# Half of a slot pair moved ahead of the row maxima, and fixed steps for the pairs of the sample attention

## What is computed

```python
h = rms_norm(x); q, k, v, u, g_att, g_s5 = split(h @ w_in)
att = softmax(q1 k1) v - lam * softmax(q2 k2) v        # 8 heads, causal; prompt, and sample over its pages
s5  = z * sigmoid(z @ w_glu + b_glu)                   # z = gelu(state space scan of u)
x   = x + (sigmoid(g_att) * (norm(att) @ w_pa) + sigmoid(g_s5) * (s5 @ w_ps)) @ w_out
# PEER: for every token and each of 8 heads, 16 experts out of 16384
h2  = rms_norm(x); s1, s2 = keys1 @ q1, keys2 @ q2      # 128 scores each; top 16 of each, top 16 of their sums
w   = softmax(best16) * gelu(dot(U[best16], h2))
x   = x + sum(w * V[best16]);  y = rms_norm(x)
```

## Time and profile before

| | |
|---|---|
| three runs | 4514.21, 4517.23, 4521.22 us |
| median | 4517.23 us |
| the profiled execution | 4512.55 us |
| its span in the trace | 4510.5 us |
| busy: PE, DVE, ACT, POOL | 74%, 67%, 33%, 30% of the span |
| DMA | 1418.40 MB, mean 314 GB/s |
| TensorE's mean granted clock | 0.90 of full speed |

### The profile page before, as it was taken

The page is one execution under the profiler, slowest core; times in us unless marked ns, Lnnn a source line. Parts: engine busy times, 40 slices in busy tenths (PEclk is TensorE's granted clock), DMA queues, the critical chain, the costliest instruction groups (busy, mean ns, idle before and its releaser), DMA issues. The chain is left out here.

```text
span 4510.5 us, 43431 instructions
## 1 busy us (share of the span) xinstructions
PE 3352.7 (74%) x13272; PEld 1915.2 (42%) x13272; DVE 3029.0 (67%) x6485; ACT 1502.6 (33%) x3882; POOL 1333.7 (30%) x1167
## 2 busy tenths in 40 slices
PE   7757979787768668877767758887777777777776
PEld 4636666543444344344456644442222222222221
DVE  6473021688887778967776667886666766666674
ACT  2121141233553214335433323323333333333332
POOL 0000000233223333422132323364444444434443
PEclk9877989898888889988878979999999999999999
DMA  3126425899878899966689989899999999999997
GB/s 128 24 1 112 148 83 179 334 377 351 283 262 340 333 393 359 405 223 224 217 320 389 402 328 395 315 397 419 420 418 412 414 412 414 410 414 397 413 409 306
DMA packets 285979, 1418.40 MB, mean 314 GB/s; under 512 B 47490, under 2 KB 89954, under 8 KB 148642
## 3 DMA queue, kind: packets, MB, share of 16 engines
q0 software_dynamic: 159344, 1129.94, 63.0%
q1 hardware_dynamic: 126018, 285.55, 18.4%
q10 hardware_dynamic: 384, 0.13, 0.0%
HBM read 1371.05 MB, written 42.11 MB: 313 GB/s over the span
## 5 line engine op out<-in xcount | busy, mean ns | idle before, releaser
L906 POOL DMA_INDIRECT arena<-in_uv,arena x1056 | 1265.2, 1198 | 2329.5 <-DVE arena L1017 1427.2
L1007 DVE CUSTOM_DVE_ANT_0 arena<-arena 128x1024 f32<-128x1024 f32 x1056 | 1289.0, 1222 | 491.0 <-DMA arena<-in_uv,arena 464.5
L1125 PE MATMUL ps<-arena 128*128 128x512 f32 (+1 forms) x2280 | 1079.0, 618 | 403.5 <-ACT arena L1094 403.5
L648 PE MATMUL ps<-arena 128*128 128x256 f32 (+2 forms) x3456 | 1111.0, 482 | 147.5 <-DMA arena<-in_w_stat 57.6
L648 PEld LDWEIGHTS ps<-arena 128*128 128x128 f32 x3456 | 685.5, 201 | 537.0 <-issue 350.3
L1125 PEld LDWEIGHTS ps<-arena 128*128 128x128 f32 (+1 forms) x2280 | 411.0, 190 | 1071.1 <-ACT arena L1094 625.0
L1075 ACT ACTIVATE arena<-arena 128x2 f32<-128x2 f32 x528 | 107.3, 203 | 1745.0 <-DVE arena L1007 1741.6
L1017 DVE SCALAR_TENSOR_TENSOR arena<-arena 128x1024 f32<-128x1024 f32 x486 | 622.3, 1280 | 10.3 <-ACT arena L1084 10.3
L1084 ACT ACTIVATE arena<-arena 128x1 f32<-128x1 f32 x1056 | 253.4, 287 | 17.6 <-ACT arena L1075 0.3
L1075 ACT ACT_TABLE_LOAD x158 | 202.7, 1283 | 10.5 <-PEq L1191 3.0
L1094 ACT ACTIVATE arena<-ident,arena 128x128 f32<-128x128 f32 x538 | 186.6, 394 | 8.8
(11 more groups left out here) (248 smaller groups left out, 3272.6 us busy)
## 6 DMA issues: line engine op xcount, KB each, us to landing
arena<-in_w_stat SPq DMA_DIRECT2D x216, 512.0 KB, 7.6
arena<-in_cache_k SPq DMA_DIRECT2D x64, 512.0 KB, 10.6
arena<-in_cache_v SPq DMA_DIRECT2D x64, 512.0 KB, 11.7
arena<-in_w_mov SPq DMA_DIRECT2D x14, 2048.0 KB, 14.3
arena<-in_uv,arena POOLq DMA_INDIRECT x1056, 13.0
arena<-in_x SPq DMA_DIRECT2D x16, 512.0 KB, 8.5
arena<-scr_s POOLq DMA_DIRECT2D x64, 128.0 KB, 12.9
scr_s<-arena SPq DMA_DIRECT2D x16, 384.0 KB, 12.0
```

The costliest lines, as they stand in the source:

```text
L648: last = nc.tensor.matmul(ps[:, bank, 0:w], wbuf[m % NWB][:, kc * P:(kc + 1) * P], moving[:, kc, :], start=(kc == 0), stop=(kc == KC - 1))
L906: pool.indirect_dma_start(ring[s % RING], None, dr["uv"], bass.IndirectOffsetOnAxis(ap=idx[:, g % 4, j:j + 1], axis=0)).then_inc(row_in[s ...
L1007: nc.vector.tensor_tensor_reduce(ring[s % RING][:, 0:D], ring[s % RING][:, 0:D], h2r[:, b % 2, :], 1.0, 0.0, ALU.mult, ALU.add, act_in[:, ...
L1125: last = nc.tensor.matmul(ps[0:m, 4 * (b % 2) + c, :], diag[:, n % 4, 0:m], ring[s % RING][:, D + 512 * c:D + 512 * (c + 1)], start=start, ...
```

## The change

Two edits. In the prompt attention a new `peer_dve_first` writes the first half of the unit's next pair (dot of slot 2p, add of slot 2(p-1)) right behind the probabilities, ahead of the maxima and of output_in; `peer_dve` later in the unit then leaves this half out. It does so in every unit, also in the last of a head, where no maxima follow. In the sample attention `share_dec` replaces `share`: five pairs per sequence of 8 steps, one each on steps 0, 1, 4, 6 and 7, so that all 40 stand on steps 0 to 63 and none behind. ScalarE's and VectorE's calls for pairs ahead of that go. GpSimd's list of pairs stays at all 40, at the start of the stage.

```diff
+        begun = {"dve": -1}
+
+        def dve_half(dve, p, q):
+            if p < PAIRS:
+                u_dot(dve, 2 * p + q)
+            if 0 < p <= PAIRS and not on_pe(p - 1):
+                v_add(dve, 2 * (p - 1) + q)
+
...
-            for q in range(2):
-                if p < PAIRS:
-                    u_dot(dve, 2 * p + q)
-                if 0 < p <= PAIRS and not on_pe(p - 1):
-                    v_add(dve, 2 * (p - 1) + q)
+            if begun["dve"] < p:
+                dve_half(dve, p, 0)
+            dve_half(dve, p, 1)
...
+        def peer_dve_first(dve, upto):
+            p = done_pairs["dve"]
+            if begun["dve"] < p < upto:
+                dve_half(dve, p, 0)
+                begun["dve"] = p
+
...
+        def share_dec(c, n):
+            before = PAIRS_BEFORE[c] + sum(PAIR_PLAN[c][:STAGES.index("dec")])
+            return before + min(PAIR_PLAN[c][STAGES.index("dec")], n // PAGES * 5 + (1, 2, 2, 2, 3, 3, 4, 5)[n % PAGES])
...
                             probabilities(h, i)
+                            peer_dve_first(dve, share(c, "att", h * nf + i + 1, H * nf))
                             if i + 1 < nf:
                                 maxima(h, i + 1)
...
-                        peer_pe(pe, share(c, "dec", n + 4, n_all))
+                        peer_pe(pe, share_dec(c, n))
...
-                    peer_act(act, share(c, "dec", 3, n_all))
...
-                        peer_act(act, share(c, "dec", n + 4, n_all))
+                        peer_act(act, share_dec(c, n))
...
-                        if n == 1:
-                            peer_dve(dve, share(c, "dec", 3, n_all))
...
-                        peer_dve(dve, share(c, "dec", n + 4, n_all))
+                        peer_dve(dve, share_dec(c, n))
...
-                    peer_pool(pool, share(c, "dec", 0, 1))
+                    peer_pool(pool, share_dec(c, N_STEPS - 1))
```

## The result

| | before | changed |
|---|---|---|
| median | 4516.40 us | 4537.46 us |
| four runs | 4514.21 to 4521.22 | 4535.84 to 4538.54 |
| profiled execution, span | 4512.55, 4510.5 us | 4538.54, 4536.6 us |

The changed kernel takes 1.0046 of the time before, with a 95% interval of 1.0031 to 1.0061: 21 us slower. The forecast of 4528 us has the right sign and lies 9 us low.

The account below looks back on a forecast made before the run. Gathers near 410 GB/s set the pace once the front stages end, so front time moves the end one for one. Attention 8 us slower plus sample stage 3 makes 11, on the median 4517.23: 4528 us, range 4490 to 4546.

Parts of the forecast that it names:

- The replay of a head: One head in the second attention stretch: new waits at the key tile's copy and for ScalarE's weights, head 2.0 us longer.
- the first stretch: First attention stage with pairs: halves overrun gaps by 1.0 us in eight heads, 8 us, less 5 back: 3 us slower.
- The second stretch: Second attention stage with pairs: later third-block maxima 5.5 us, weights' wait 4.5, some 5 given back: 5 us slower.
- Only 0.8 us of the 2.4 are won: First query block of the replayed head: the half fits the gap, but the rest becomes a wait at the key tile's copy.
- rival 1: Attention: VectorE is the bound, so its filled gaps are time won, about 25 us: 4495 us; chance 0.17.
- Block 3's half: Third query block of a head: its add waits for ScalarE's weights, some 0.6 us a head, 4.5 us in all.
- Part 2: Sample stage edit: loop to the last softmax 16 us longer, last steps 13 us shorter, together 3 us slower.
- 5 us for filled gaps: Sample loop: a fixed set of pairs around each sequence boundary fills part of the transfer gaps, 5 us less.
- the mark that I had set as a sign of being wrong: Sample loop: a mean DMA rate above 410 GB/s would show the forecast wrong.
- 2 (the loop has room): Sample loop: boundary pairs fill all transfer gaps, the loop pays little and the end gives 13 us: 4512 us; chance 0.20.
- 3 (the loop pays in full): Sample loop: eight rows asked for at once and late key pages make it 17 us slower: 4542 us; chance 0.13.
- 4 (part 1 does nothing): Attention edit: what is filled reappears as waits of the same size: 4520 us; chance 0.10.

Follow-up runs that it names:

- after_fill: Changed kernel plus ten unread identity products on TensorE ahead of the turned outputs, in all heads but first and last of the two attention stretches: 0.9979 of before.
- before_fill: Kernel before plus the same ten unread identity products on TensorE ahead of the turned outputs, nothing else: 0.9991 of before.
- half_b1: Kernel before plus the attention edit only at the first of a head's three query blocks, ahead of the second block's maxima: 0.9947 of before.
- half_b3: Kernel before plus the attention edit only at a head's third query block, ahead of the last output read: 1.0012 of before.
- att_only: Kernel before plus the whole attention edit, with the sample stage of before: 1.0042 of before.
- b1_fill_two: b1_fill plus eight more unread products ahead of the second query block's scores, where TensorE waits for the exponentials: 0.9930 of before, 4490.3 us.
- dec_only: Kernel before plus the sample edit alone, with the attention of before: 0.9996 of before.
- b1_dec37: half_b1's attention, with 37 of the 40 sample pairs in steps 0 to 63 and three behind: 0.9943 of before.
- b1_even64: half_b1's attention, with all 40 sample pairs spread evenly over steps 0 to 63, no set steps: 0.9945 of before.
- b1_fill: half_b1 plus six unread identity products on TensorE ahead of the turned outputs: 0.9948 of before.
- half_b2: Kernel before plus the attention edit only at a head's second query block, ahead of the third block's maxima: 1.0052 of before.

## Why the prediction was right in sign and 9 us low

**What bounds the kernel, and that front time moves the end one for one:** right. The four stretches differ by 24.9 us and the spans by 26.1.

**The replay of a head:** right in its mechanism. The new waits stand where it put them: L1575 does wait (6.0 us in the second stretch, where the kernel before had no such wait behind its first maxima; 5.8 in the first, 1.8 before), and L1017 waits 29.2 and 19.2 us. Their size at L1017 was more than double, 48.4 us in both stretches for "about 20", and the 9.4 that the prediction gives for before is the second stretch alone (10.2 in both). The slower query tile ahead of ScalarE's weights is part of that: with the fill in, L1017 waits 26.1 us in `after_fill` and 7.4 in `before_fill`. In the head of the earlier trace rows the key tile's copy is 0.8 us earlier and block 3's maxima are 1.15 us later, forecast 0.8 and 1.3; the head got 3.5 us longer for a forecast 2.0, and the query tile's 1.3 us are most of the difference.

**The term that was mis-sized is the first stretch, +3 us in the sum and +18.8 measured.** It was made of an overrun of 1.0 us in eight heads, 8 us, less 5 that a busy VectorE would give back. The overrun came: block 3's maxima stand 11.5 us later there, summed over eight heads, each counted from its own first maxima. The step that failed is that I had kept every duration of TensorE at its value in the trace of before: its 770 products took 15.6 us more (195.5 for 179.9), at a lower granted clock. 5.3 of these lie in the six query tiles behind the longer wait, the rest in other products, whose cause no run isolates. With the query tiles at full clock in both (`after_fill` against `before_fill`) 8.2 of the 18.8 us are left, still with slower other products in it, so whether VectorE gave the 5 us back can't be read from these runs.

**The second stretch, +5 forecast and +4.6 measured,** is a hit by luck. With the fill in both, 334.3 stands against 336.8, no loss that can be told from zero where I had 5; the fill takes 13.3 us off the changed kernel and 6.2 off the kernel before, and the forecast had nothing of that.

**"Only 0.8 us of the 2.4 are won" at block 1:** right for the head that I replayed, wrong as a verdict on block 1. `half_b1` gains 24 us, nearly the 25 us that rival 1 had for the whole edit. I had ruled the rival out by the wait ahead of the query tile of one head. In five of the eight heads in which VectorE is late at block 3, with top-k steps ahead of it, the half is time won, and I had counted these as heads in which nothing moves. The prediction replayed the three halves as one chain and so never asked what each would do alone.

**Block 3's half, some 4.5 us for the weights' wait in the second stretch:** the wait came, its price didn't. In the second stretch of `half_b3` the waits for weights rise from 9.4 to 13.7 us, but the waits for outputs fall from 15.7 to 10.3, and the stretch is 0.1 us longer. The 4.6 us lie in the first stretch, where I had named no such wait; that the total fits is an accident.

**Part 2:** the loop +11.5 us for +16, the last steps -10.0 for -13, the sum +1.5 for +3; in time, nothing that can be measured. My 5 us for filled gaps was too small: the mean rate rose from 398 to 410 GB/s, just to the mark that I had set as a sign of being wrong. No pair stands in the last steps, as forecast, where the window 2678 to 2704 has VectorE busy for 3.63 us. The large wait for the last scores fell from 49.5 to 17.1 us; the one for the turned probabilities rose from 29.1 to 38.5.

**The rivals:** 2 (the loop has room) is half right by the mean rate but gave no gain in time. 3 (the loop pays in full) is out, at +11.5. 4 (part 1 does nothing) is out by `att_only`.

A note on precision: each stretch is read from one profiled execution, which lies up to 9 us from its kernel's median (`b1_fill_two`: 4499.6 for 4490.3). The attention stretches repeat better than that: the three kernels with block 1's half and no added products have 254.1 to 255.5 and 329.6 to 331.9 us, `dec_only` and before 263.4 and 263.3, 340.6 and 343.0. A difference of up to 2.5 us between stretches is therefore no finding, and verdicts rest on the ratios.

## What to carry to other kernels

Filling an engine's idle gap helps only where that engine is what is late next: try a moved piece of work at each of its places alone, for here one place gains 24 us, one loses 23, and the sum hides both. When you replay a trace with a delay in it, ask of each longer idle on TensorE whether the products behind it were at full clock, and price them at the slow rate too. The best versions found, `b1_fill_two` (0.9930), `b1_dec37` (0.9943), `b1_even64` (0.9945), `half_b1` (0.9947) and `b1_fill` (0.9948), all keep only block 1's half; their intervals overlap.

## What the runs showed of the hardware

A wait of some 3 us on TensorE cost more than its own length: in the changed kernel and `half_b2` the sixteen products behind it took 6.4 to 8.4 us for 5.33 or 5.75 in 23 of 24 heads, at a granted clock of 0.67 and 0.76 in the two windows shown. It isn't a fixed rule of the wait. In the changed kernel one head has 3.34 us of idle and a tile of 5.33 us behind it; in the kernel before, one has 0.54 us of idle and a tile of 7.56. Filling a part of the wait with products that nobody reads (2.40 of 3.82 us) was enough to keep every query tile behind it at full clock in three kernels. By the ratios this was worth 30 us in the changed kernel, 17 in `half_b2` (both give or take some 10), and next to nothing in the kernel before.
